# Value products in front of score products, transposes behind them, and index scores in fours

## The reference

```python
# indexer of the sparse attention, per block of 128 queries
dots = jnp.einsum('bqhd,bsd->bqhs', qi_blk, ki)
score = jnp.einsum('bqhs,bqh->bqs', jax.nn.relu(dots), wi_blk)
...
# both causal attentions of the first block (a: keys picked by the indexer; b: decay c)
logits = q.k * scale (+ c_q - c_k in b), masked causally
probs = jax.nn.softmax(logits, axis=-1)
out = jnp.einsum('bhqs,bshd->bqhd', probs, v)
...
# odd layer: each query sees a window of its neighbourhood and the 256 context keys
p = softmax(concat([q.k_window + bias, q.k_context]))
out = p_w @ v_window + p_c @ v_context
```

## Time and profile before

| | us |
|---|---|
| median of 3 runs | 1340.55 (1338.69 to 1341.50) |
| the profiled execution | 1339.49 |
| its span, first to last instruction | 1337.7 |
| PE matmul busy in the span | 1260.2 (94%) |
| DVE busy | 679.5 (51%) |
| ACT busy | 623.7 (47%) |
| POOL busy | 459.1 (34%) |

### The profile page before, as it was taken

The page is one execution under the profiler, slowest core; times in us unless marked ns, Lnnn a source line. Parts: engine busy times, 40 slices in busy tenths (PEclk is TensorE's granted clock), DMA queues, the critical chain, the costliest instruction groups (busy, mean ns, idle before and its releaser), DMA issues.

```text
span 1337.7 us, 19533 instructions
## 1 busy us (share of the span) xinstructions
PE 1260.2 (94%) x7148; PEld 997.3 (75%) x7148; DVE 679.5 (51%) x1287; ACT 623.7 (47%) x1336; POOL 459.1 (34%) x360
## 2 busy tenths in 40 slices
PE   7999999999999989869999999999988999999998
PEld 6877776776788767668878788787766878677776
DVE  4666965655414244185747757714604701665353
ACT  6544326655533254262256666626325422655533
POOL 4534343321344343451233333322342033221342
PEclk9999999999999999879999999999999999999999
DMA  6421541110442643440232220011163141221442
GB/s 226 132 71 63 190 158 63 36 40 28 157 141 92 255 154 126 155 176 1 91 111 91 80 103 33 32 64 64 34 234 127 47 152 70 64 96 64 157 130 91
DMA packets 28429, 140.33 MB, mean 105 GB/s; under 512 B 4304, under 2 KB 5712, under 8 KB 15728
## 3 DMA queue, kind: packets, MB, share of 16 engines
q1 hardware_dynamic: 21584, 117.72, 25.1%
q10 hardware_dynamic: 6752, 21.35, 4.8%
HBM read 122.74 MB, written 6.29 MB: 96 GB/s over the span
## 4 chain that ended last, share of the span: by engine, by line
PE 72%; DVE 11%; ACT 7%; issue 3%; DMA 3%; POOL 3%; ACTq 1%; DVEq 0%; SPq 0%; POOLq 0%
PE psum L643 46%; PE psum L671 5%; DMA w_raw<-stream 3%; PE psum L775 2%; POOL w_low L1182 2%; DVE arena L2203 2%; PE psum L999 2%; ACT w_high L1358 2%; DVE small L2200 2%; PE psum L866 2%; PE psum L1167 2%; PE psum L631 1%; PE psum L983 1%; PE psum L975 1%; DVE arena L2021 1%
## 5 line engine op out<-in xcount | busy, mean ns | idle before, releaser
L1182 POOL TENSOR_TENSOR w_low<-w_raw,w_high 128x512 fp32r<-128x512 f32 x264 | 353.6, 1354 | 705.8 <-ACT w_high L1358 705.6
L1358 ACT CAST w_high<-w_raw 128x512 fp32r<-128x512 f32 x264 | 157.9, 622 | 324.8 <-PE psum L643 166.5
L643 PE MATMUL psum<-x_high,w_high 128*128 128x512 f32 x528 | 222.6, 422 | 6.6 <-POOL w_low L1182 2.4
L643 PE MATMUL psum<-x_low,w_high 128*128 128x512 f32 x528 | 208.0, 394 | 0.0
L643 PE MATMUL psum<-x_high,w_low 128*128 128x512 f32 x528 | 207.4, 393 | 0.0
L643 PEld LDWEIGHTS psum<-x_high,w_high 128*128 128x128 f32 x528 | 99.8, 189 | 50.1 <-issue 24.5
L643 PE MATMUL psum<-w_high,x_high 128*128 128x512 f32 x288 | 116.4, 404 | 15.0 <-ACT w_high L1358 9.2
L643 PEld LDWEIGHTS psum<-x_high,w_low 128*128 128x128 f32 x528 | 100.0, 189 | 22.4
L643 PE MATMUL psum<-w_high,x_low 128*128 128x512 f32 x288 | 113.4, 394 | 0.0
L643 PE MATMUL psum<-w_low,x_high 128*128 128x512 f32 x288 | 113.4, 394 | 0.0
L643 PEld LDWEIGHTS psum<-x_low,w_high 128*128 128x128 f32 x528 | 100.2, 190 | 16.2 <-issue 0.7
(11 more groups left out here) (454 smaller groups left out, 2677.9 us busy)
## 6 DMA issues: line engine op xcount, KB each, us to landing
w_raw<-stream SPq DMA_DIRECT2D x98, 1024.0 KB, 4.9
x_kept<-arena ACTq DMA_DIRECT2D x8, 512.0 KB, 4.8
arena<-x_kept ACTq DMA_DIRECT2D x8, 512.0 KB, 5.4
arena<-bias ACTq DMA_DIRECT2D x8, 512.0 KB, 3.8
q_masked<-e_q_high SPq DMA_DIRECT2D x24, 96.0 KB, 2.5
arena<-x SPq DMA_DIRECT2D x4, 512.0 KB, 5.2
arena<-x ACTq DMA_DIRECT2D x4, 512.0 KB, 6.2
arena<-ctx ACTq DMA_DIRECT2D x4, 512.0 KB, 6.8
```

What stands on the lines that cost most here:

```text
L643: mm = pe.matmul(o, l, r, start=(first and n == 0 and kind != "fc"), stop=(last and n == len(passes) - 1))
L1182: pool.tensor_tensor(PLACE[u][1], RAW[:, g % 2, u % 4, :], PLACE[u][0].bitcast(F32), ALU.subtract).then_inc(w_lo, 1)
L1358: act.copy(PLACE[u][0], RAW[:, g % 2, u % 4, :]).then_inc(w_hi, 1)
```

## The change

In the index loop two pairs of scores are made back to back, then the pieces of all four numbers follow. The pieces are as many as before, and ACT and DVE keep their order.

In the causal loop and the near loop an even step is now V, S, T, F and an odd step T, F. A value product comes one step later than before, directly in front of the scores of that step, and the transpose of an even step stands behind the scores. ACT's copies of the value products move one step (causal) or two steps (near) later in its own order.

```diff
-            for i in range(0, len(INDEX), 2):
-                pr, t, _ = INDEX[i]
-                ...
-                for n in (i, i + 1):
+            for first in range(0, len(INDEX), 4):
+                for i in (first, first + 2):
+                    pr, t, _ = INDEX[i]
+                    ...
+                for n in range(first, first + 4):
                     feed("i", pieces, n_pieces * (n + 1) // 24 - n_pieces * n // 24)
...
             for s in range(len(BOTH) + 7):
+                if s >= 8 and s % 2 == 0:
+                    values_both((s - 8) // 2)
+                if s < len(BOTH) and s % 2 == 0:
+                    score_both(s)
                 if 4 <= s < len(BOTH) + 4:
                     turn_both(s - 4)
-                if s < len(BOTH) and s % 2 == 0:
-                    score_both(s)
-                if s >= 7 and s % 2:
-                    values_both((s - 7) // 2)
...
-            for s in range(steps + 4):
+            for s in range(steps + 5):
+                if s >= 6 and s % 2 == 0:
+                    values_near((s - 6) // 2)
+                if s < steps and s % 2 == 0:
+                    score_near(s // 2)
                 if 2 <= s < steps + 2:
                     turn_near(s - 2)
-                if s < steps and s % 2 == 0:
-                    score_near(s // 2)
-                if s >= 5 and s % 2:
-                    values_near((s - 5) // 2)
...
-                if s >= 8 and s % 2 == 0:
-                    values_both((s - 8) // 2)
+                if s >= 9 and s % 2:
+                    values_both((s - 9) // 2)
...
-                if s >= 5 and s % 2:
-                    values_near((s - 5) // 2)
+                if s >= 7 and s % 2:
+                    values_near((s - 7) // 2)
```

More of the change, by code:

```diff
@@ L805, in _ @@
             pieces, n_pieces = stream("qb", "kb"), 2 * 4 * NK
-            for i in range(0, len(INDEX), 2):
-                pr, t, _ = INDEX[i]
[L808 to L811, removed]
-                for n in (i, i + 1):
+            for first in range(0, len(INDEX), 4):
+                for i in (first, first + 2):
+                    pr, t, _ = INDEX[i]
+                    w = P * (t + 1)
+                    b = (i + 2) % 4
+                    score_pair([("i", i), ("i", i + 1)], (b, b + 1), prep_of("i", pr), t,
+                               BH[:, 1, 0:w], BL[:, 1, 0:w])
+                for n in range(first, first + 4):
                     feed("i", pieces, n_pieces * (n + 1) // 24 - n_pieces * n // 24)
@@ L1920, in _ @@
             steps = ATT["n"].steps
-            for s in range(steps + 4):
+            for s in range(steps + 6):
                 for c in ("gn0", "gn1", "gd0", "gd1"):
```

## The result

| | median, us | lowest to highest |
|---|---|---|
| before | 1341.50 | 1338.69 to 1344.59 |
| after | **1330.43** | 1327.58 to 1335.44 |

The ratio is 0.9916, with a 95% interval from 0.9896 to 0.9936. The forecast was 1326.0 with a range from 1319 to 1331. The sign and the range held; the median lies above the band that the prediction called its own forecast, 1323 to 1328. The gain is 11 us where 14.5 were forecast. One execution further down, of kernel 5, took 2193 us at a granted clock of 0.75 and is left out of the times given there.

A forecast was written before the change was run, and what follows sets the result against it. TensorE was taken to set the time, through its order and few waits. Terms -6.4 - 0.5 - 3.1 - 4.9 + 0.4 = -14.5 gave 1325.0 us for the profiled execution, 1326.0 against the median; range 1319 to 1331.

The forecast's parts named there:

- the price of a change of kind, also from V to S: TensorE, all loops: exit into F or T 0.21 us, entry into S 0.20, into V 0.14; V to S one change.
- Rivals B: Causal and near loops: V to S costs between nothing and half a change, 1317.4 to 1321.7 us; chance 0.08.
- C (double): Causal and near loops: V to S costs two changes, one through the whole array, 1334.6 us; chance 0.06.
- The two waits: Index loop: TensorE waits for ACT at scores 10 and 22, 1.65 us each, 3.3 in all.
- Forecast -6.9: Causal loop: 6.4 us saved in changes of kind and 0.5 in the third transpose's wait.
- S exits into T instead of F at the same price: Causal loop: leaving scores for a transpose costs the same as leaving them for pieces, 0.21 us.
- my bound of 4: Causal loop, attention a: DVE's max of even maps comes 0.3 to 0.6 us later; taken as 0, at most 4.
- Rival F: Causal loop: the order moves but DVE's later max gives back up to 4 us, 1330 us; chance 0.05.
- the waits of the near loop: Near loop: 14 waits of odd transposes (2.8 us) go, and long ones shrink by 1.3, 0.4 and 0.4; together 4.9.
- rivals A: Index loop: the clock falls in the new waits at scores 10 and 22, 1327.7 to 1329.4 us; chance 0.20.
- One sign of being wrong: In the loops of the profile after: a granted clock under 1.0 would show the prediction wrong.
- Rival E: Near loop: the clock falls after each of 13 joined stretches, 22 us more, 1348 us; chance 0.03.

The follow-up runs named there:

- kernel 5: The changed kernel, but index scores of the groups from 6 and 18 are read in plain order; 1324.72, 1324.88 and 1330.47 us, ratio 0.9884.
- only causal: The kernel before with only the causal loop changed, index and near loops left old; 1334.89 us, ratio 0.9939.
- kernel 9: The changed kernel, with ACT's copy of value products in front of the exponential in the causal loop; 1330.6 us in a single execution.
- 10: The changed kernel, with plain order of index sums in groups from 6 and 18 and ACT's copy before the exponential in near and causal loops; 1322.16 us.
- Kernel 6: The changed kernel, with ACT's copy of a value product in front of the exponential in the near loop; 1333.0 us in a single execution.
- kernel 8: The changed kernel, with the even transpose put back between value product and scores in causal and near loops; 1343.8 us in a single execution.

## Why the prediction was right, and where it was off

**Right: the price of a change of kind, also from V to S.** It was the open price, taken as one change, and it is one, at all 41 places. Rivals B (cheap) and C (double) fall with that. The Trainium skill, "TensorEngine Tiling (Array Packing)", under "Key Properties", says that changing the tiling mode drains the engine. The trace agrees: the start gap goes from 0.10 to 0.20, or from 0.23 to 0.32, at every change, be it from one half mode to the other or to the whole array, and the load behind it costs up to 0.11 on top.

**Right: the index loop.** Forecast +0.4, measured +0.4. The two waits cost 1.62 each (forecast 1.65), and the piece behind the joined scores is idle for 0.52 where the earlier trace rows have 1.05 (forecast 0.5 less).

**Right by offsetting sizes: the causal loop.** Forecast -6.9, measured -6.3 without a fall. Two terms were off, each the other way.
- The step "S exits into T instead of F at the same price" was wrong, to my favour. A transpose behind S takes 0.41 to the piece, one behind a piece 0.36 (1198.29 to 1198.70, 1200.18 to 1200.54 above); so an exit into T is 0.16, an exit into F 0.21. That is 0.05 in each of the 16 periods of attention a, 0.8.
- New waits for which I took 0. In the trace of only causal: 0.26 in front of a value product, 0.30 of a transpose, 0.20 of scores, and at the loop's end 2.46 where before had 1.61. There the third last value product waits for ACT's copy of the one before, as kernels 9 and 10 showed. Together 1.6 more. They were inside my bound of 4, but not the max of DVE that I had named. ACT's copy of the value product, one step later in its order, is the cause of half of it: putting it in front gave 0.8 back (kernel 9), the rest stays open. The 0.30 is a copy of DVE's behind two scalings of 512 columns that took 1.61 and 1.44 us there, with GpSimd at work for 1.3 and 1.2 us of that; the same scaling takes 0.49 us at 309.63, where GpSimd is idle.

With these the sum is -6.4 - 0.5 - 0.8 + 1.6 = -6.1, measured -6.3. That the forecast total came so near is luck in part: the two errors happen to offset.

Rival F, DVE's later max, is therefore not seen as what gave time back.

**Wrong: the waits of the near loop.** Forecast -4.9, measured -0.8, and this term is nearly all of the miss. Summed by start gaps, before had 5.3 us of waits and lost loads behind its entry, after has 4.5. I had taken the old waits away one by one, and that held: of 5.3 only 0.8 is left, at two transposes, where I expected 0.5. What I did not do is ask, for the moved value product, who frees its bank. I asked it for the transposes (bank 4, ACT's copy, "it fits") and not for bank 5, though the text on the change says that ACT's copies move by two steps. There a step was missing from the sum: with the copy behind the exponential the next value product is 2.6 late in all (0.3, 0.3, 1.0, 0.4, 0.6), and two pieces are 1.0 late for the gates' copies, which stand in the same queue. Kernel 6 gave 1.7 of it back by one exchange. At the measured price the changes of kind there gave 3.1, as forecast, and the cheaper exit into T 0.7 more. Sum: -3.1 - 0.7 - 0.8 = -4.6, measured -4.75.

**The median.** The stages without falls give +0.4 - 6.3 - 4.75 = -10.7. The medians give -11.1, with an interval of some 2.7 either way, so that they meet within 0.4 is luck. The forecast had -14.5; of the 3.8 between it and the stages the near loop is 3.25 and the causal loop 0.6. The median of 1330.43 is outside the forecast of 1323 to 1328. It is inside the range only because that reached up to 1331 for rivals A and F, and neither is why the time came out there: no fall followed the waits of the index loop in the profile of after, and F is not seen. The range held for a reason that the prediction did not have.

One sign of being wrong did show: a granted clock under 1.00 in the causal loop, 6.8 us at its end. The old loop had it too in two of three profiles, so it does not speak against the change.

**Rival A** had its mechanism, idle then half the clock, in one of five profiles with that wait, at 1.6 us, and never behind the second wait, at scores 22. I gave it 0.20. **Rival E** (falls in the joined stretches) has nothing for it: no near loop, joined or not, had a clock under 1.00.

## What to carry to other kernels

Count TensorE's changes between whole-array and half-array matmuls, and put kinds of halves side by side: each exit avoided gave some 0.2 us here (0.18 where 28 of them were taken back in kernel 8), and none of it shows as a wait. When an operation moves, ask who frees its output bank, and what stands in front of that freeing copy in its own engine's order. Such a copy in front of an exponential instead of behind it gave 1.7 and 0.8 us here. With the plain order of the index sums, 3.5, that is 6 us more in the stages: from 10.7 to 16.7. The medians say 11 and 21, part of it by luck with the clock.

## What the runs showed of the hardware that I had not expected

- The second matmul behind a change starts late too, by 0.11 us among pieces and by 0.055 among transposes: an exit into pieces costs 0.21, into transposes 0.16, though both load 128 columns.
- The lower clock comes in the same few places in every profile (582.8 to 596.4 in after, 582.9 to 596.6 in before), and in others only now and then: at the end of the causal loop with an old and a new order, at 1070 and 1292 us. Executions of one kernel differ by up to 13 us, as much as the gain: before took from 1335.97 at a granted clock of 0.985 to 1348.94 at 0.977. A profile is one such draw: the two profiled executions differ by 4 us, the stages without falls by 11.
- A wait of 1.46 us behind 0.6 us of scores was followed by the lower clock once in five profiles. What decides it here stays open.
- DVE's scaling of 128x512 floats takes 0.49 us alone and up to 1.61 us while GpSimd works (1.3 us of overlap). In the trace of after all 25 of that size without GpSimd beside them took 0.49, and all 12 over 0.6 us had 0.36 us or more of GpSimd work in them.
